# A hybrid streaming encoder step on one core: operands loaded into the low parts' place, norm scaled ahead of its copies, one partial kept over each change of phase, sums built further apart

## The chip, the cores and the metric

The kernel runs on one core of one Trainium2 chip. The metric is device time in microseconds of one execution; lower is better. All inputs, weights and results are float32.

## The reference, cut to what matters

```python
def layer(x, pool_buf, conv_buf, offset, ...):
    h = rmsnorm(x, norm_g)                       # x: 1024 + 64 tokens, D = 2048
    proj = einsum('btd,dc->btc', h, w_in)        # 2048 x 10240
    xa, za, v, bg, cg, zb, ga, gb = split(proj)  # 6 x 1024, 2 x 2048 columns
    ya, new_pool = pool_mixer(xa, ...)           # trailing means, small linear map
    ya = ya * silu(za)
    yc, new_conv = conv_mixer(cg * v, ...)       # three taps
    yb = bg * yc * silu(zb)
    merged = sigmoid(ga + b) * (ya @ w_proj_pool) + sigmoid(gb + b) * (yb @ w_proj_conv)
    return x + merged @ w_out, new_pool, new_conv
y = rmsnorm(layer(x), final_norm_g)
```

## The kernel before

All large products have the tokens on the free axis: weights are the stationary operand, activations (feature on the partition, 1,088 tokens) the moving one. To reach float32 accuracy each matrix is split into a high part (rounded to the fast float32 format) and a low part (the rest), and a product is three matmuls: high by high, high by low, low by high.

**Seven products for eight.** The work goes in pairs, numbered g = 0 to 111. A pair is 256 output columns by 1,024 (8 x 128) rows of weights. It is treated as a 2 x 2 block product and computed with seven block products instead of eight (q = 0 to 6), whose operands are sums and differences of blocks. So there are 784 products, s = 7g + q. A product is 24 matmuls of 272 tokens; in the last two phases 12 matmuls of 384.

**Phases.** H0 (g 0 to 39) and H1 (40 to 79) are the two halves of the input projection's rows: H0's results are partial sums, stored to memory (`part`) and loaded again in H1. H1's pairs also carry the pooling, convolution and gate work. YA (80 to 87) and YB (88 to 95) are the two branch projections, M0 (96 to 103) and M1 (104 to 111) the two halves of the output projection for the first 768 tokens, again with a partial result in memory (`part_m`). A tail T of 64 products of 12 matmuls of 320 tokens does the last 320 tokens without the seven-for-eight scheme.

**Operands of a phase.** The seven moving operands of a phase stand in SBUF as `ops` (H0 to YB) or `opm` (M0, M1), each with a high and a low half. At a change of phase they are all replaced, while the last pair of the old phase still uses them one by one. Three are plain blocks (`rawq`), four are sums (`sumq`) which "builds" make ahead of time: SyncE loads a quarter into `tb_in`, VectorE makes four differences into `tb_out` (`build`), GpSimd stores them; each build waits for the store of the one before. At the change SyncE loads operand o into one of two staging buffers (`load_operand`, `stage` or `stm`), ScalarE rounds it into the high half (`operand_hi`, L927), VectorE subtracts into the low half (`operand_lo`, L1171). The load of operand o + 2 waits for the low part of operand o:

```python
if o < 2:
    sp.wait_ge(tb_stored, 16 * BUILT[YB if ph == YA else ph])
    sp.wait_ge(ops_lo, NQ * (ph - 1) + NQ)
else:
    sp.wait_ge(ops_lo, k - 1)
```

**Order of the work.** Every engine runs one list, written by hand, in order of s. At position s ScalarE drains product s - 1 if it is its turn, and makes the high part of the weights of product s + 3; VectorE drains product s - 1 (L1164, all seven of a pair in H1 and M1, three in the others), makes the low part of the weights of s + 3 (L1118) and the weight sum of s + 4 (L1137), then whatever else is scheduled there. TensorE starts product s when its weights are split, its operand is there, and product s - 2 is drained. SyncE issues nearly all loads in one list of its own, GpSimd the stores. Each waits in order: whoever waits holds up all behind it.

**Buffers.** Three 8.7 KB-per-partition result buffers `pb` form a ring, `ring(g)`: g mod 3 up to H1, then g mod 2; `pbm` has two in M0 and M1. A buffer may be written when the store of its last content has landed. In YA and YB the third one holds gates (`gate`).

**The start.** For each of nine token tiles ScalarE squares the rows (L1050), VectorE makes the variance (L1394), GpSimd the inverse root (`rstd`), VectorE scales (L1401), TensorE turns the tile (L802, 16 transposes into four PSUM areas), ScalarE copies the first half out (`copy_first`, L1043) and VectorE the second (`copy_second`, L1389). Both copies of tile t stand ahead of the scaling of tile t + 1. Then come the first operands: `first_operand_sum`, `first_operand_hi`, `first_operand_lo` (L1184, L939, L1188).

**The end.** In M1 each pair's result is turned back (`turn_back`), added to x (`sum_columns`) and squared (`square_columns`, six squares of ScalarE at position q = 4), and at q = 5 of four pairs a quarter of the last tokens' operand `opb` is rounded (L1079) and subtracted (L1435). After product 783 SyncE loads the last rows of x (`res`), the final norm's vector (`fin_g`), and then goes on with the weights of T.

Of the kernel before, what the change touches and what calls it, by code (L numbers as in the profile page):

```python
# [10 lines left out]
P = 128  # L11
# [4 lines left out]
def bass_hybrid_stream_step(nc, x_prompt, x_sample, state_pool, state_conv, norm_g, w_in, b_gate,  # L16
# [25 lines left out]
    KQ = 4  # L42
# [58 lines left out]

    def ring(g):
        return g % 3 if g < FIRST[YA] else g % 2

    stored_after, n_stored = {}, [0, 0, 0]
    for g in range(FIRST[M1]):
        ph, j = phase(g), g - FIRST[phase(g)]
        if ph == H1:
            k = {"gate": 1, "za": 2, "zb": 2}.get(KIND[j], 0)
        else:  # L110
            k = {H0: 1, YA: 1, YB: 3, M0: 1}[ph]
        n_stored[ring(g)] += 16 * k
        stored_after[g] = n_stored[ring(g)]

    with ExitStack() as ctx:
# [31 lines left out]
        ops = at("ops", 0, [NQ, KQ, 2, TH], F32R)  # L147
        pb = [at(f"pb{k}", PB0 + k * PB_B, [2, TOK]) for k in range(3)]
# [23 lines left out]
        t0 = at("t0", PB0 + KE * TOK * 4, [KQ, TH])  # L172
# [4 lines left out]
        opm = at("opm", 0, [NQ, KQ, 2, AH], F32R)  # L177
        opb = at("opb", OPM_B, [KD, 2, B], F32R)
        PBM0 = OPM_B + KD * 2 * B * 4
        pbm = [at(f"pbm{k}", PBM0 + k * 2 * A * 4, [2, A]) for k in range(2)]  # L180
        assert PBM0 + 2 * 2 * A * 4 <= PB0 + 2 * PB_B
        xcol = [at(f"xcol{k}", (PB0 + 2 * PB_B, DS0)[k], [AT, 2 * P]) for k in range(2)]
        sqj = at("sqj", DS0 + AT * 2 * P * 4, [2 * P])
        stm = [at(f"stm{k}", (XE0, WS0)[k], [KQ, AH]) for k in range(2)]
        tbm_in = at("tbm_in", XE0, [4, AH])
        tbm_out = at("tbm_out", WS0, [4, AH])
        stb = [at(f"stb{k}", (XE0, WS0)[k], [KQ, B]) for k in range(2)]
        res = at("res", 0, [BT, D])
        ob = at("ob", BT * D * 4, [2, B])
        fin = [at(f"fin{k}", (BT * D * 4 + 2 * B * 4, WS0)[k], [D]) for k in range(2)]  # L190
        fin_g = at("fin_g", XE0, [D])
# [47 lines left out]
        def out_tile(g):  # L239
            return pb_first if g == 0 else pbm[g % 2] if g >= FIRST[M0] else pb[ring(g)]  # L240
# [8 lines left out]
        def operand(ph):  # L249
            return ops if ph < M0 else opm  # L250
# [42 lines left out]
        stage_landed = [sem(f"stage_landed{k}") for k in range(2)]  # L293
# [39 lines left out]
        stb_landed = [sem(f"stb_landed{k}") for k in range(2)]  # L333
# [69 lines left out]
        BUILD = [(FIRST[H0] + 4 + k, 3, H1, k) for k in range(KQ)]  # L403
        BUILD += [(FIRST[H1] + GB0 + 1 + k // 2, 2 + 3 * (k % 2), (YA, YB)[k // KQ], k % KQ) for k in range(2 * KQ)]
        BUILD += [(FIRST[YB] + 5 + k // 2, 2 + 3 * (k % 2), M0, k) for k in range(KQ)]
        BUILD += [(FIRST[M0] + 2 + k, 3, M1, k) for k in range(KQ)]
        BUILT = {ph: sum(p <= ph for _, _, p, _ in BUILD) for ph in range(6)}

        SOURCE = ((0, 0), (1, 0), (1, 1), (0, 3), (1, 2), (0, 2), (1, 3))

# [6 lines left out]
        for g in range(NP):  # L417
            if is_partial(g):
                n_landed[ring(g)] += 16
                landed_after[g] = n_landed[ring(g)]  # L420
# [13 lines left out]
        def _(sp):  # L434
# [19 lines left out]
            def load_partial(g):  # L454
                ph, j = phase(g), g - FIRST[phase(g)]
                if ph == H1:
                    before = g - 3
                    kind, i = (KIND[j - 3], (j - 3 - CONV0) // 4) if j >= 3 else ("gate", 0)
                    if kind == "xa":
# [7 lines left out]
                    sp.wait_ge(pb_stored[ring(j)], stored_after[j])  # L467
                    sp.dma_start(pb[ring(g)][:, :, :].rearrange("p c t -> p (c t)"), part[j]) \
                        .then_inc(pb_landed[ring(g)], 16)
                else:  # L470
                    if j < 2:
                        sp.wait_ge(pb_stored[ring(g)], stored_after[g - 2])
# [1037 lines left out]
```

## Time and profile before

| | |
|---|---|
| median of 3 runs | 2656.14 us (2653.65 to 2657.09) |
| the profiled execution | 2653.98 us |
| its span, first to last instruction | 2652.2 us |
| TensorE busy | 2487.2 us, 94% |
| VectorE, ScalarE, GpSimd busy | 1600.6, 888.3, 106.5 us |
| mean granted TensorE clock | 0.973 |
| DMA, mean over the span | 163 GB/s |

The span is what the trace covers; 1.8 us of the execution's time lie around it. TensorE's busy time contains stretches in which it ran at half its clock, so the distance to an undisturbed run is more than the 6% of idle time.

### The profile page before, as it was taken

How to read it: one execution, taken by the hardware profiler on the slowest of the kernel's cores; microseconds unless marked ns; L12 is line 12 of the kernel's file. 1: busy time of each engine (PE TensorE's matmuls, PEld its weight loads, DVE VectorE, ACT ScalarE, POOL GpSimd, SP SyncE). 2: the span in 40 equal slices, each digit the busy share in tenths (PEclk: the TensorE clock that was granted, in tenths of full speed). 3: DMA queues.
4: the chain of work that ended last, by engine and by line, in shares of the span. 5: the costliest groups of instructions: out<-in, count | busy, mean ns of one | idle time of the engine just before them, and what ended most of it. 6: DMA issues, size and time to landing. Idle time of an engine off the chain costs nothing.

```text
span 2652.2 us, 44708 instructions
## 1 busy us (share of the span) xinstructions
PE 2487.2 (94%) x18737; PEld 2474.6 (93%) x18737; DVE 1600.6 (60%) x2311; ACT 888.3 (33%) x1493; POOL 106.5 (4%) x201
## 2 busy tenths in 40 slices
PE   4799999999999989999999999889998996989987
PEld 3799999999999989999999999889998996989887
DVE  4745444444444476777777687666556666667654
ACT  4433333333333333323322222224334323444354
POOL 1000000000000000000000000000000010000000
PEclk9899999999999989999999999989999998989999
DMA  4345333333233444343333333785447585667686
GB/s 176 116 131 202 111 111 99 104 102 99 99 111 112 151 177 150 120 153 137 141 107 116 116 116 111 255 285 216 151 161 272 200 282 195 215 222 245 216 270 186
DMA packets 216013, 433.63 MB, mean 163 GB/s; under 512 B 9684, under 2 KB 168724, under 8 KB 196295
## 3 DMA queue, kind: packets, MB, share of 16 engines
q1 hardware_dynamic: 191222, 291.70, 33.1%
q0 software_dynamic: 23648, 132.27, 13.4%
q10 hardware_dynamic: 944, 6.82, 0.7%
q8 instruction: 149, 2.44, 0.4%
q14 instruction: 50, 0.40, 0.0%
HBM read 295.87 MB, written 134.88 MB: 162 GB/s over the span
## 4 chain that ended last, share of the span: by engine, by line
PE 81%; DMA 8%; DVE 6%; issue 3%; ACT 2%; POOL 0%; SPq 0%; DVEq 0%; ACTq 0%; POOLq 0%
PE ps L785 77%; DMA stage<-sumq 1%; DMA raw<-in_w_out_dram 1%; PE ps L886 1%; DMA stm<-sumq 1%; DMA sumq<-tb_out 1%; PE ps L802 1%; PE ps L815 1%; ACT ops L927 1%; DVE ops L1171 1%; DMA tbm_in<-rawq 1%; DMA tb_in<-rawq 1%; DVE xn L1401 1%; DVE tb_out L1208 1%; ACT sqj L1018 1%
## 5 line engine op out<-in xcount | busy, mean ns | idle before, releaser
L785 PE MATMUL ps<-ops,hi 128*128 128x272 f32 x10752 | 1807.4, 290 | 71.5 <-DVE pb L1164 53.5
L785 PEld LDWEIGHTS ps<-ops,hi 128*128 128x128 f32 x10752 | 1544.6, 191 | 75.3 <-issue 75.3
L785 PE MATMUL ps<-ops,lo 128*128 128x272 f32 x5376 | 1121.0, 290 | 0.0
L785 PEld LDWEIGHTS ps<-ops,lo 128*128 128x128 f32 x5376 | 847.5, 190 | 0.0
L1164 DVE TENSOR_TENSOR pb<-pb,ps 128x544 f32<-128x544 f32 x429 | 308.9, 720 | 382.6 <-PE ps L785 381.5
L907 ACT ACTIVATE hi<-sb 128x512 fp32r<-128x512 f32 x448 | 283.7, 633 | 637.7 <-PE ps L785 555.5
L1118 DVE TENSOR_TENSOR lo<-raw,hi 128x512 fp32r<-128x512 f32 x400 | 275.5, 689 | 298.0 <-ACT hi L907 295.8
L1118 DVE TENSOR_TENSOR lo<-sb,hi 128x512 fp32r<-128x512 f32 x448 | 308.2, 688 | 204.2 <-ACT hi L907 202.6
L907 ACT ACTIVATE hi<-raw 128x512 fp32r<-128x512 f32 x400 | 252.8, 633 | 480.5 <-PE ps L785 420.2
L920 ACT COPY pb<-ps 128x544 f32<-128x544 f32 x220 | 134.8, 613 | 416.0 <-PE ps L785 415.9
L785 PE MATMUL ps<-opm,hi 128*128 128x384 f32 x896 | 234.8, 343 | 27.2 <-DVE pbm L1164 17.3
L785 PEld LDWEIGHTS ps<-opm,hi 128*128 128x128 f32 x896 | 164.3, 193 | 30.7 <-issue 30.3
L1137 DVE TENSOR_TENSOR sb<-raw 128x512 f32<-128x512 f32 x224 | 153.4, 685 | 0.0
L785 PE MATMUL ps<-opm,lo 128*128 128x384 f32 x448 | 152.4, 340 | 0.0
L886 PE MATMUL ps<-opb,hi 128*128 128x320 f32 x512 | 115.9, 315 | 0.0
L886 PEld LDWEIGHTS ps<-opb,hi 128*128 128x128 f32 x512 | 86.6, 191 | 0.0
L785 PEld LDWEIGHTS ps<-opm,lo 128*128 128x128 f32 x448 | 86.1, 192 | 0.0
L886 PE MATMUL ps<-opb,lo 128*128 128x320 f32 x256 | 79.9, 312 | 0.0
L1137 DVE TENSOR_TENSOR sb<-sb,raw 128x512 f32<-128x512 f32 x112 | 76.7, 685 | 0.0
L1137 DVE TENSOR_TENSOR sb<-raw,sb 128x512 f32<-128x512 f32 x112 | 76.7, 685 | 0.0
L1171 DVE TENSOR_TENSOR ops<-stage,ops 128x2176 fp32r<-128x2176 f32 x21 | 50.9, 2423 | 26.3 <-ACT ops L927 26.3
L802 PE MATMUL ps<-ident,xn 128*128 128x128 f32 (+1 forms) x144 | 30.7, 406 | 32.3 <-DVE xn L1401 32.3
(121 smaller groups left out, 1030.7 us busy)
## 6 DMA issues: line engine op xcount, KB each, us to landing
raw<-in_w_in_dram SPq DMA_DIRECT2D x160, 512.0 KB, 3.8
pb<-part SPq DMA_DIRECT2D x40, 1088.0 KB, 6.8
part<-pb POOLq DMA_DIRECT2D x39, 1088.0 KB, 5.0
raw<-in_w_out_dram SPq DMA_DIRECT2D x64, 512.0 KB, 4.4
gates<-pb POOLq DMA_DIRECT2D x16, 1088.0 KB, 8.7
gate<-gates SPq DMA_DIRECT2D x32, 544.0 KB, 8.3
tb_in<-rawq SPq DMA_DIRECT2D x12, 1088.0 KB, 8.1
sumq<-tb_out POOLq DMA_DIRECT2D x12, 1088.0 KB, 9.6
```

What stands on the lines that cost most here:

```text
L785: mm = nc.tensor.matmul(ps[b][:, c, 0:n], w[:, s % R, kt * P:(kt + 1) * P], t[:, q, kt, half, k * n:(k + 1) * n], start=fresh and kt == 0 ...
L802: mm = nc.tensor.transpose(flat[b][:, k * P:k * P + r], xn[0:r, t, (a * KE + k) * P:(a * KE + k + 1) * P], ident[0:r, 0:r])
L815: mm = nc.tensor.matmul(ps[3][:, jb, 0:HC], w[:, kt, jb * P:(jb + 1) * P], ds[:, kt, half, :], start=kt == 0 and w is mix_hi and half == 0 ...
L886: mm = nc.tensor.matmul(ps[0][:, cb % 2, 0:B], w[:, n % R, kt * P:(kt + 1) * P], opb[:, kq * KQ + kt, half, :], start=kq == 0 and kt == 0 ...
L907: nc.scalar.activation(split_of(hi, n), src, ACT.Copy).then_inc(w_hi, 1)
L920: nc.scalar.copy(target(s), psum(s)).then_inc(act_drained, 1)
L927: nc.scalar.copy(operand(ph)[:, o, :, 0, :], (stage if ph < M0 else stm)[slot][:, :, :]) \
L1018: nc.scalar.activation(sqj[:, :], xcol[j % 2][:, t, :], ACT.Square, accum_out=sums_a[:, t, j:j + 1]).then_inc(squared, 1)
L1118: nc.vector.tensor_tensor(split_of(lo, n), src, f32(split_of(hi, n)), ALU.subtract).then_inc(w_lo, 1)
L1137: nc.vector.tensor_tensor(sb_of(g, q), a, b, op).then_inc(s_made, 1)
L1164: nc.vector.tensor_tensor(target(s), target(s), psum(s), ALU.add).then_inc(dve_drained, 1)
L1171: nc.vector.tensor_tensor(t[:, o, :, 1, :], src, f32(t[:, o, :, 0, :]), ALU.subtract).then_inc(ops_lo, 1)
```

## The change

1. **Operands load into place.** The staging buffers go. `ops_raw[o]` and `opm_raw[o]` are float32 views of the operands' own memory, and an operand is loaded where its low half will stand (rows of 544 or 384 values, one out of two). Its load waits only for the old phase's product o, and the last operand's load for the last product. Rounding starts four positions after, the subtraction, now in place, five: one operand at each position (`HI_LAG`, `LO_LAG`). `opb` is done in the same manner.
2. **The start.** `variance` of tile t + 1 stands ahead of the scaling of tile t, and the copies of tile t - 2 behind it; the first operand is rounded and subtracted before the last tile's copies, whose tokens it does not hold. The second and third operands' sums get memory of their own, so that one need not wait for the use of the other. The stores of `h1raw` start with the tokens that are ready.
3. **One partial kept.** The last pair of H0 and of M0 computes the same columns as the first of H1 and M1 (`position`, `is_kept`), and its result stays in its buffer instead of going out and in. `ring` is shifted to fit: g mod 3 in H0, (g - 1) mod 3 in H1, and it starts at 0 in YA, YB and M0. `pbm` moves to other memory.
4. **Builds further apart.** The eight builds of YA and YB stand 5 products apart (before 3 and 4 in turn), those of M0 4 apart (before 3 and 4). `tb_in` and `tb_out` have other places in M1.
5. **The end.** The six squares are spread in twos over q = 4, 5, 6, the rounding of `opb` moves to q = 1, `fin_g` is loaded in M1, the last rows from the second product of the last pair on.

```diff
     def ring(g):
-        return g % 3 if g < FIRST[YA] else g % 2
+        ph = phase(g)
+        if ph in (H0, H1):
+            return (g - (ph == H1)) % 3
+        return (g - FIRST[ph] + (ph == M1)) % 2
...
+        BUILD = [(NQ * (FIRST[H0] + 4 + k) + 3, H1, k) for k in range(KQ)]
+        BUILD += [(NQ * (FIRST[H1] + GB0 + 1) + 2 + 5 * k, (YA, YB)[k // KQ], k % KQ) for k in range(2 * KQ)]
+        BUILD += [(NQ * (FIRST[YB] + 5) + 4 * k, M0, k) for k in range(KQ)]
+        BUILD_LOAD_AT = {max(s - 3, BUILD[e - 1][0] + 1 if e > 0 else 0): e for e, (s, _, _) in enumerate(BUILD)}
+        HI_LAG, LO_LAG = 4, 5
...
             def load_operand(ph, o):
+                if o == 0:
+                    sp.wait_ge(tb_stored, 16 * BUILT[ph])
+                sp.wait_ge(product_done, NQ * (FIRST[ph] - 1) + o + 1)
                 kind, i = SOURCE[o]
+                sp.dma_start(operand(ph)[1][o][:, :, 1, :], (sumq if kind else rawq)[ph][:, i, :, :]) \
+                    .then_inc(ops_landed[o], 16)
...
+            def load_last_rows():
+                sp.wait_ge(product_done, NS - NQ + 2)
...
                 if q == 0:
+                    if g == FIRST[M0]:
+                        act.wait_ge(tb_made, 4 * BUILT[M0])
+                    elif stored_before[g] > 0:
+                        act.wait_ge(pb_stored[ring(g)], stored_before[g])
...
+            variance(0)
+            dve.wait_ge(g_landed, 16)
+            for t in range(TT):
+                if t + 1 < TT:
+                    variance(t + 1)
                 dve.wait_ge(rstd_made, t + 1)
                 nc.vector.scalar_tensor_tensor(xn[0:r, t, :], ...).then_inc(x_scaled, 1)
+                if t > 1:
+                    copy_second(t - 2)
```

VectorE's list at the start of the program, before the change (`xn` is the tile, `h1raw` the second half's copy out of PSUM):

```order
3 L1394 TENSOR_SCALAR var<-ssq 128x1
4 L1401 SCALAR_TENSOR_TENSOR xn<-xn,rstd,gbc 128x2048
5 L1394 TENSOR_SCALAR var<-ssq 128x1
6 L1389 COPY h1raw<-ps 128x8x128
7 L1401 SCALAR_TENSOR_TENSOR xn<-xn,rstd,gbc 128x2048
```

And VectorE's list at the same place with the change:

```order
3 L1419 TENSOR_SCALAR var<-ssq 128x1 x2
4 L1429 SCALAR_TENSOR_TENSOR xn<-xn,rstd,gbc 128x2048
5 L1419 TENSOR_SCALAR var<-ssq 128x1
6 L1429 SCALAR_TENSOR_TENSOR xn<-xn,rstd,gbc 128x2048
7 L1419 TENSOR_SCALAR var<-ssq 128x1
8 L1429 SCALAR_TENSOR_TENSOR xn<-xn,rstd,gbc 128x2048
9 L1414 COPY h1raw<-ps 128x8x128
```

Three tiles are scaled ahead of the first copy, where before a copy stood between any two; the second variance now stands ahead of the first scaling.

SyncE's list around the change from H0 to H1, before the change (`stage` are the staging buffers, `raw` the weights, `pb` the partial results):

```order
18 L490 DMA stage_63<-rawq 128x2176
19 L490 DMA stage_64<-sumq 128x2176
20 L447 DMA raw<-in_w_in_dram 128x4x256
21 L468 DMA pb_51<-part 128x2176
22 L490 DMA stage_63<-sumq 128x2176
23 L490 DMA stage_64<-rawq 128x2176
24 L447 DMA raw<-in_w_in_dram 128x4x256
25 L490 DMA stage_63<-sumq 128x2176
26 L490 DMA stage_64<-rawq 128x2176
27 L490 DMA stage_63<-sumq 128x2176
```

And SyncE's list at the same place with the change (`ops_raw` are the operands' own places):

```order
18 L516 DMA ops_raw_50<-rawq 128x4x544
19 L516 DMA ops_raw_51<-sumq 128x4x544
20 L516 DMA ops_raw_52<-sumq 128x4x544
21 L475 DMA raw<-in_w_in_dram 128x4x256
22 L516 DMA ops_raw_53<-rawq 128x4x544
23 L516 DMA ops_raw_54<-sumq 128x4x544
24 L516 DMA ops_raw_55<-rawq 128x4x544
25 L475 DMA raw<-in_w_in_dram 128x4x256
26 L498 DMA pb_58<-part 128x2176
27 L516 DMA ops_raw_56<-sumq 128x4x544
```

The load of pair 40's partial (21 before) is gone; each operand load stands behind one product of the old phase instead of the low part two before it, is made of rows of 544 values instead of one run of 2,176, and the last one stands behind the load of pair 41's partial.

## Rows read from the trace of the kernel before

**Rows 1.** The chain that ended last, four of its pieces: start, length, what.
```profile
111.52 809.35 PE ps L785 x6432
...
926.47 6.26 DMA stage<-sumq
932.75 2.02 ACT ops L927
...
2507.11 15.27 DMA raw<-in_w_out_dram
```

**Rows 2.** Stretch of M0, L785 alone: length, PE busy (matmuls), clock, DMA share, GB/s.
```profile
2247.00:2340.00 93.00, 93.00 (x537) 1.00 0.61 205
```

**Rows 3.** As rows 2, for L886, two stretches of the tail T.
```profile
2505.00:2534.00 29.00, 17.34 (x102) 0.82 0.84 278
2534.00:2563.00 29.00, 28.67 (x191) 1.00 0.95 284
```

**Rows 4.** TensorE's waits: us in total, times, longest.
```profile
PE ps L785 <- DVE pb L1164: 53.5, 14, 10.3
```

**Rows 5.** As rows 2, stretches with waits in them.
```profile
929.00:965.00 36.00, 26.65 (x177) 0.81 0.66 240
1671.00:1790.00 119.00, 103.46 (x760) 0.91 0.77 275
1829.00:1868.00 39.00, 30.41 (x225) 0.96 0.72 257
2016.00:2048.00 32.00, 23.16 (x169) 0.89 0.70 247
2160.00:2225.00 65.00, 49.59 (x355) 0.87 0.79 282
2226.00:2247.00 21.00, 11.12 (x50) 0.76 0.32 111
2348.00:2380.00 32.00, 20.25 (x90) 0.79 0.74 249
2402.00:2473.00 71.00, 62.13 (x342) 1.00 0.65 223
```

**Rows 6.** The timeline of the start: start, length, instruction, idle before it.
```profile
13.77 1.91 ACT L1050 ACTIVATE junk<-xn 128x2048 f32<-128x2048 f32 x1 [5.81 <-DMA xn<-in_x_prompt_dram]
...
24.86 1.23 DVE L1389 COPY h1raw<-ps 128x1024 f32<-128x1024 f32 x1 [3.71 <-PE ps L802]
26.00 2.34 DVE L1401 SCALAR_TENSOR_TENSOR xn<-xn,rstd,gbc 128x2048 f32<-128x2048 f32 x1
...
28.40 3.68 PE L802 MATMUL ps<-ident,xn 128*128 128x128 f32 x16 [3.58 <-DVE xn L1401]
...
78.73 1.25 PE L785 MATMUL ps<-ops,hi 128*128 128x272 f32 x4 [5.50 <-DVE ops L1188]
```

**Rows 7.** The page: costliest groups (busy, mean ns) and DMA issues (us to landing).
```profile
L1164 DVE TENSOR_TENSOR pb<-pb,ps 128x544 f32<-128x544 f32 x429 | 308.9, 720 | 382.6 <-PE ps L785 381.5
...
L1118 DVE TENSOR_TENSOR lo<-sb,hi 128x512 fp32r<-128x512 f32 x448 | 308.2, 688 | 204.2 <-ACT hi L907 202.6
...
L1171 DVE TENSOR_TENSOR ops<-stage,ops 128x2176 fp32r<-128x2176 f32 x21 | 50.9, 2423 | 26.3 <-ACT ops L927 26.3
...
gates<-pb POOLq DMA_DIRECT2D x16, 1088.0 KB, 8.7
...
tb_in<-rawq SPq DMA_DIRECT2D x12, 1088.0 KB, 8.1
sumq<-tb_out POOLq DMA_DIRECT2D x12, 1088.0 KB, 9.6
```

**Rows 8.** Stretches of all engines: PE, PEld, DVE, ACT, POOL busy; clock, DMA share, GB/s.
```profile
10.00:15.00 5.00, 1.31 (x7) 1.20 (x7) 2.84 (x4) 1.23 (x1) 0.56 (x1) 1.00 1.02 424
...
194.00:201.00 7.00, 7.00 (x58) 7.00 (x57) 4.87 (x8) 1.56 (x3) 0.20 (x1) 1.00 0.87 269
```

**Rows 9.** The timeline of TensorE in pair 107 of M1.
```profile
2420.05 0.59 PE L785 MATMUL ps<-opm,hi 128*128 128x384 f32 x2 [1.40 <-DVE pbm L1164]
```

More of the change, by code:

```diff
@@ L147, in bass_hybrid_stream_step @@
         ops = at("ops", 0, [NQ, KQ, 2, TH], F32R)
+        ops_raw = [at(f"ops_raw{q}", q * KQ * 2 * TH * 4, [KQ, 2, TH]) for q in range(NQ)]
         pb = [at(f"pb{k}", PB0 + k * PB_B, [2, TOK]) for k in range(3)]
@@ L164, in bass_hybrid_stream_step @@
         so = at("so", DS0, [E])
+        tb_in = {ph: at(f"tb_in{ph}", XE0 if ph < M1 else WS0, [4, TH if ph < M0 else AH])
+                 for ph in (H1, YA, YB, M0, M1)}
+        tb_out = {ph: at(f"tb_out{ph}", WS0 if ph < M1 else DS0, [4, TH if ph < M0 else AH])
+                  for ph in (H1, YA, YB, M0, M1)}
         xn = at("xn", 0, [TT, D])
@@ L239, in out_tile @@
         def out_tile(g):
-            return pb_first if g == 0 else pbm[g % 2] if g >= FIRST[M0] else pb[ring(g)]
+            return pb_first if g == 0 else pbm[ring(g)] if g >= FIRST[M0] else pb[ring(g)]
         def target(s):
@@ L249, in operand @@
         def operand(ph):
-            return ops if ph < M0 else opm
+            return (ops, ops_raw) if ph < M0 else (opm, opm_raw)
         V_B, V_S, V_W = 0, 2 * KD, 2 * KD + KE
@@ L292, in bass_hybrid_stream_step @@
         ops_lo = sem("ops_lo")
-        stage_landed = [sem(f"stage_landed{k}") for k in range(2)]
+        ops_landed = [sem(f"ops_landed{k}") for k in range(NQ)]
         tb_landed = sem("tb_landed")
@@ L417, in bass_hybrid_stream_step @@
         for g in range(NP):
-            if is_partial(g):
+            if is_partial(g) and not is_kept(g - 1):
                 n_landed[ring(g)] += 16
@@ L454, in load_partial @@
             def load_partial(g):
-                ph, j = phase(g), g - FIRST[phase(g)]
+                ph, j = phase(g), position(g)
                 if ph == H1:
                     before = g - 3
-                    kind, i = (KIND[j - 3], (j - 3 - CONV0) // 4) if j >= 3 else ("gate", 0)
-                    if kind == "xa":
+                    kind, i = (KIND[j - 3], (j - 3 - CONV0) // 4) if j >= 3 else (None, 0)
+                    if j < 3:
+                        sp.wait_ge(pb_stored[ring(g)], stored_after[g - 4])
+                    elif kind == "xa":
                         sp.wait_ge(dve_drained, dve_count[NQ * before + 6])
@@ L622, in _ @@
-            sp.wait_ge(product_done, NS)
-            for t in range(BT):
-                sp.dma_start(res[0:rows(AT + t), t, :], x_rows(AT + t)).then_inc(res_landed, 16)
-            sp.wait_ge(opb_lo, KQ)
-            sp.dma_start(fin_g[:, :], final_norm_g.rearrange("(a d) -> a d", a=1).broadcast_to([P, D])) \
-                .then_inc(fin_g_landed, 16)
+                if q == 0:
+                    load_weights(2 * g + 3)
+                    if ph == M1:
+                        load_x_columns(j)
+                    if ph == H1 and j < CONV0 and j % 4 == 1:
+                        load_mix(j // 4)
+                    if g + 1 < NP and is_partial(g + 1) and not is_kept(g):
+                        load_partial(g + 1)
@@ L682, in store_pair @@
             def store_pair(g):
-                ph, j, k = phase(g), g - FIRST[phase(g)], ring(g)
+                ph, j, k = phase(g), position(g), ring(g)
+                if is_kept(g):
+                    return
                 if ph == H0:
@@ L1011, in input_post, with square_columns @@
                                 .then_inc(conv_tails, 1)
-            def square_columns(j):
+            def square_columns(j, tiles=range(AT)):
                 act.wait_ge(summed, 2 * j + 2)
-                for t in range(AT):
+                for t in tiles:
                     if AT * j + t > 0:
@@ L1389, in copy_second, with variance @@
                 nc.vector.tensor_copy(h1raw[:, :, t * P:t * P + r], src).then_inc(h1_copied, 1)
-            for t in range(TT):
+            def variance(t):
                 r = rows(t)
```

311 lines of the change are left out of this document (148 added, 163 removed).

## The prediction, made before the changed kernel was run

> **What bounds the kernel now.** I read the time table first: TensorE is busy 94% of the span, so the kernel is TensorE's work plus what TensorE loses. Then the chain of work that ended last: from 111.52 us on it is one piece of 809.35 us of TensorE, 6,432 matmuls, so an undisturbed matmul of 272 tokens costs 809.35 / 6,432 = 0.1258 us and a product of 24 costs 3.02 [rows 1]. In M0 an undisturbed matmul costs 93.00 / 537 = 0.1732, a product 2.08 [rows 2], in the tail 29.00 / 191 = 0.152 with its transposes [rows 3]. Third, TensorE's waits: 53.5 us in 14 waits for a result to be drained [rows 4]. They stand at few places, so I took stretches around them and counted matmuls. What a stretch is longer than its matmuls' undisturbed time is its loss, waits and slow clock together [rows 5]:
>
> - H0 to H1, 929 to 965: 36 - 177 x 0.1258 = 13.7
> - builds for YA and YB, 1671 to 1790: 119 - 95.6 = 23.4
> - H1 to YA: 39 - 28.3 = 10.7
> - YA to YB: 32 - 21.3 = 10.7
> - builds for M0 and the change to M0: 65 - 44.7 = 20.3 and 21 - 50 x 0.1732 = 12.3, together 32.6
> - M0 to M1: 32 - 15.6 = 16.4
> - M1, pairs 106 to 109: 71 - 59.2 = 11.8
> - start of T: 29 - 102 x 0.152 = 13.5 [rows 3]
>
> The clock is in these numbers: in the first stretch the engine was idle 36 - 26.65 = 9.35 us, yet 13.7 were lost; the granted clock of the stretch was 0.81, that is, part of it stood at 1.2 GHz instead of 2.4 after the waits. I price a wait of some us at its length plus 2 us.
>
> **The start.** Now each tile is a cycle: scaling 2.34, turning 3.68, copy 1.23, one after the other, so that TensorE idles 3.58 before each 3.68 of turning [rows 6]: 7.26 us a tile, nine tiles. With two scalings ahead, turning and VectorE's work (about 3.6 a tile) overlap and the turning bounds, say 3.74. Against that, the second variance now stands ahead of the first scaling, and needs tile 1: its squares start at 13.77, when the tile lands, and take 1.91 and some 0.2 to read the sum out [rows 6]. So the first scaling ends near 18.3, the nine turns (the last one half as long) near 50. VectorE is then still at: two copies to 50, a weight sum and the first operand's low part to 53, five weight steps of 0.6 and the last copy to about 57, where product 0 starts; now it starts at 78.73 [rows 6]. Products 1 to 6 come at the pace of the operands in both versions: per operand a rounding 2.0, a low part 2.42 and a sum 2.4. Walking both engines' new lists with these durations, I get products 1 to 6 at 66, 71, 75, 82, 86, 90; the present chain has product 6 at 111.52 [rows 1]. **Gain 22.** Bounds: 15, if the turns run 0.5 slower and the operands' order costs a wait, to 26.
>
> **Changes of phase.** Now staging, rounding and low part form a chain: 6.26 for the load, 2.02, 2.42 [rows 1, 7]: 10.7 for every second operand. That chain goes. Next is VectorE: in seven positions in a row it has a low part 2.42, a weight low part 0.69, 4/7 of a weight sum, and 6/7 of a drain 0.72 [rows 7], about 3.9 us with the overlap of issue, against 3.02. The list allows it about 2 us of lateness (a low part is made two positions ahead: 6.0 - 3.9). So 7 x 3.9 - 7 x 3.02 - 2 = 4 us of waiting, plus 2 to 2.5 of clock: **6.5 for H0 to H1, gain 7.2.**
>
> The loads themselves: each consists of 512 rows of 2,176 bytes. No load before has that destination; the nearest is `tb_in`, with rows of the same length. Alone with little else it had 269 GB/s at a busy share of 0.87, so 309 when full; whole rows moved at 424 [rows 8]. Seven operands, two weight loads, a partial in and one out are 11.1 MB: 26 us at 424 GB/s, 36 at 309. From the first load to the need for the last low part there are 12 products, 36.1 us, less 6.4 for latency, rounding and low part: 29.7, and with VectorE's stall 33.7. So at the fast rate nothing is added, at the slow one 2 to 6 us at each of three changes. I take 0, as both queues together had 282 GB/s averaged over 65 us with pauses in it [rows 5], and keep 6 for the range. The Trainium skill, page "DMA: Bandwidth & Descriptors", section "Where 436 GB/s comes from", says that for HBM to SBUF the HBM side binds at about 358 GB/s per core. By that, 11.1 MB would take 31 us and each of three changes about 1 us more, the result some 3 us later than mine. The 424 GB/s of the row stands against it as a hard bound.
>
> **H1 to YA: gain 0.** Here the new `ring` puts pair 80 into the buffer of pair 79 (before: of 78). ScalarE's first drain in YA must wait for pair 79's gates to be stored. From the start of pair 80: VectorE is 2.4 late, drain 0.7, sigmoid of 1,088 values 1.2 (as the copy of 1,024 values [rows 6]), issue 0.5, store 8.7 to landing [rows 7]: 13.5. Product 2 needs the drain at 6.0: 7.5 of waiting plus 0.6, 0.6 and the clock 2: 10.7, what is lost now. Behind this drain ScalarE holds roundings and weights of the next products, but those have slack. From a gain of 5 (the store lands after 5 us) to a loss of 5.
>
> **YA to YB: gain 5.2.** As H0 to H1, with three drains but two merges of 1.2: 5.5 remain.
>
> **Builds: gain 20.4.** Each waits for the store of the one before, 9.6 us, and for its own load, 8.1, which starts only when the one before is made [rows 7]. With 2.7 for the build and 0.6 to issue that is a cycle of 13 to 14; it stood 9.05 and 12.1 apart and will stand 15.1 apart. 3 us are left for some load that stands behind a pair's weights and partial in SyncE's list.
>
> **M0: gain 20.1.** Builds 12.1 apart with a cycle of 13.2 (smaller rows): three times 1.2 late, 3 in all. At the change, VectorE has low parts of 1.7, four merge steps of 1.2, two drains, weights: 25.3 us against 2 x 3.02 + 5 x 2.08 and 4 of slack, by position 6.7, plus 2 to 3 of clock. The wait of ScalarE's first drain for the last store of YB goes, since `pbm` moves. 12.5 remain of 32.6.
>
> **M0 to M1: gain 9.1.** VectorE 3 us a position against 2.08: 4.8 of waiting, 2.5 of clock: 7.3 remain.
>
> **M1: gain 5.6.** Four waits of 1.40 [rows 9], in which the low part of `opb` waited for six squares and a rounding. Six other microseconds there are the turns back, which stay. **T: gain 12.** Now the weights stand behind `res` and `fin_g` and take 15.27 to land [rows 1]. Then `res` is issued a pair's half earlier, `fin_g` long before; I leave 1.5, as ScalarE needs these weights within about 9 us.
>
> The kept partials save two stores and two loads, which nothing waited for: 0.
>
> **Sum:** 22 + 7.2 + 0 + 5.2 + 20.4 + 20.1 + 9.1 + 5.6 + 12 = 101.6. The profiled execution took 2653.98; less 101.6 that is 2552.4. The median of the runs lies 2.2 above it: **2554**.
>
> **Rivals.**
> - *The phase changes are bound by the loads.* For it: the rate of `tb_in`, and that seven loads now crowd into 30 us. Against: the 424 GB/s. It gives 6 more at three changes and 3 at the two of M0 and M1: 2578. Chance 0.18.
> - *TensorE hardly waits at the changes.* If VectorE's slack is larger than 2 us, only the gate store and a little remain, 17 instead of 42.5: 2529. Against it: a position's 3.9 us are sums of measured durations. 0.09.
> - *The builds' cycle stays late.* If loads and stores, with operands and gates beside them, take 13 us and not 10, each of twelve builds is still 1 to 3 late and the loads of the phase after with them: 2554 + 20 + 15 = 2589. 0.06.
> - *Slower.* The loads into place, one queue, do not overlap: 8.1 each [rows 7]. Seven then take 57 against 30, 27 of waiting at five changes, 135 plus clock against the 42.5 of my sum: 2657, no change; with the 9.6 of `sumq` 37 each, 2709. It decides for slower from about 8.3 us a load. Against it: 282 GB/s over 65 us is 4 us for 1.1 MB. 0.03, and 0.02 for the point between.
> - My forecast, 2536 to 2570: 0.62.
>
> **Range and chances.** 2536 to 2584 holds my case and most of the first rival. A change of 0.2%, 5 us, is about what a measurement of this kernel tells from none. Only the last rival reaches that: faster 0.95, same 0.02, slower 0.03.
>
> **What the profile after would show.** Product 0 near 57 us, product 6 near 90. At H0 to H1 no staging loads in the chain, VectorE without gaps, waits of TensorE under 5 us. At the start of YA one wait of 6 to 8 us, ScalarE behind the gates' store. No wait over 2 us in the builds' pairs. In M1 no waits of 1.40. No 12 us gap at the second block of T. I am wrong if ScalarE's roundings wait for `ops_raw` (first rival), or if new waits stand in T when its first one no longer gives the loads time.

## The result, and the profile of the changed kernel

The changed kernel took 2591.05 us (2586.20 to 2592.78, 4 runs), the kernel before beside it 2654.89 us (2646.17 to 2657.09, 4 runs): a ratio of 0.9767, 95% interval 0.9752 to 0.9781. That is faster by 2.3%, and 37 us later than forecast, outside the range. The profiled execution took 2591.84, its span is 2590.1 against 2652.2 before: 62.1 us less, where the sum had 101.6. Of all runs below one, of experiment 8, took 4011.94 us at a granted clock of 0.558 in place of 0.99, and is left out of its median.

First the stretches that answer to those of [rows 2, 3, 5], for the matmuls of the products (L812, before L785) and then for those of the tail (L913, before L886); the columns are length, TensorE busy (matmuls), TensorE's weight loads, clock, DMA share, GB/s:

```profile
897.00:945.00 48.00, 44.83 (x351) 44.06 (x351) 1.00 0.68 254
1642.00:1762.00 120.00, 111.76 (x854) 111.19 (x854) 0.96 0.72 259
1781.00:1836.00 55.00, 46.69 (x351) 46.11 (x350) 0.91 0.65 242
1967.00:2018.00 51.00, 42.75 (x307) 42.07 (x306) 0.90 0.81 300
2101.00:2180.00 79.00, 68.13 (x511) 67.53 (x509) 0.94 0.80 282
2180.00:2204.00 24.00, 17.95 (x82) 17.00 (x83) 0.86 0.55 194
2219.00:2286.00 67.00, 59.57 (x340) 58.37 (x339) 1.00 0.59 204
2300.00:2342.00 42.00, 33.26 (x175) 31.35 (x175) 0.96 0.74 254
2357.00:2421.00 64.00, 60.72 (x339) 57.91 (x337) 1.00 0.70 251
...
2453.00:2482.00 29.00, 25.75 (x168) 24.53 (x168) 1.00 0.98 309
```

Each length less its matmuls at 0.1258, 0.1732 or 0.152 us, as in the prediction, gives the loss:

| place | lost before | forecast | lost after | gain forecast | gain found |
|---|---|---|---|---|---|
| start, to product 6 | | | | 22 | 20.2 |
| H0 to H1 | 13.7 | 6.5 | 3.8 | 7.2 | 9.9 |
| builds for YA, YB | 23.4 | 3 | 12.6 | 20.4 | 10.8 |
| H1 to YA | 10.7 | 10.7 | 10.8 | 0 | -0.1 |
| YA to YB | 10.7 | 5.5 | 12.4 | 5.2 | -1.7 |
| builds for M0, and the change | 32.6 | 12.5 | 14.7 + 9.8 | 20.1 | 8.1 |
| builds for M1 | 0 [rows 2] | 0 | 8.3 | 0 | -8.3 |
| M0 to M1 | 16.4 | 7.3 | 11.7 | 9.1 | 4.7 |
| M1, four pairs | 11.8 | 6.2 | 5.3 | 5.6 | 6.5 |
| start of T | 13.5 | 1.5 | 3.5 | 12 | 10.0 |
| sum | | | | 101.6 | 60.1 |

So some 41 us of the forecast are missing, and nearly all of it stands at builds and at three changes of phase (YA to YB, to M0, to M1). What ends last there is seen in the chain that ended last (start, length, what):

```profile
91.28 821.40 PE ps L812 x6528
...
1668.78 13.24 DMA tb_in<-rawq
1689.68 12.31 DMA tb_in<-rawq
...
1808.29 8.10 DMA gates<-pb
...
1993.28 11.84 DMA ops_raw<-sumq
...
2109.51 12.30 DMA tb_in<-rawq
...
2161.27 13.28 DMA opm_raw<-rawq
...
2222.19 5.78 DMA tb_in<-rawq
...
2321.91 10.17 DMA opm_raw<-sumq
```

One piece of TensorE now reaches from 91.28, in the first pair, to 912.68, in the last pair of H0; before it reached from 111.52 to 920.87 [rows 1]. At the change into H1 the chain goes through VectorE's work alone, with no load. At the later changes and the builds it goes through loads of 6 to 13 us. Only the `gates` store was foreseen. What stands ahead of two of them in SyncE's list is read from the timeline, first at the first pair of YB, with ScalarE's rounding that waits for the load:

```profile
1991.83 0.37 SPq L475 DMA_DIRECT2D raw<-in_w_proj_conv_dram  x1
1992.30 0.45 SPq L550 DMA_DIRECT2D gate<-gates  x1
1992.85 0.38 SPq L562 DMA_DIRECT2D ma<-part_a  x1
1993.28 0.43 SPq L516 DMA_DIRECT2D ops_raw<-sumq  x1
...
2005.14 2.02 ACT L953 CAST ops<-ops_raw 128x2176 fp32r<-128x2176 f32 x1 [5.27 <-DMA ops_raw<-sumq]
```

and at a build of pair 75:

```profile
1688.72 0.37 SPq L475 DMA_DIRECT2D raw<-in_w_in_dram  x1
1689.19 0.45 SPq L498 DMA_DIRECT2D pb<-part  x1
1689.68 0.53 SPq L539 DMA_DIRECT2D tb_in<-rawq  x1
...
1702.02 1.36 DVE L1233 TENSOR_TENSOR tb_out<-tb_in 128x544 f32<-128x544 f32 x2 [5.76 <-DMA tb_in<-rawq]
```

The wanted load was issued within 1.5 us of three or two others and landed 11.84 and 12.31 us later. ScalarE then stood 5.27 us and VectorE 5.76 us, each with drains of TensorE's results behind it in its list.

The first of these loads was also issued late. TensorE had done the old phase's last product, and with it the place was free, at 1983.63; the load went out at 1993.28, 9.7 us after. What SyncE waited for in between (who, for whom; us in total, times, longest):

```profile
SPq L475 <- DVE sb L1161: 9.3, 1, 9.3
```

L475 is the load of the new pair's weights, which stands ahead in the list and waits until VectorE has made the weight sums out of the same buffer. So being behind another load has two prices: the wait of that load, which holds up SyncE's whole list, and the time in which its bytes move.

### The profile page after: what moved, and what is told of

It is laid out like the page before. It is cut to its first block, busy times and chain, and to the rows that moved or that the text cites. A ratio compares the mean times of both kernels' runs of the same rounds, so it can differ in the third digit from the quotient of the medians.

```text
span 2590.1 us, 44672 instructions
## 1 busy us (share of the span) xinstructions
PE 2469.5 (95%) x18737; PEld 2455.7 (95%) x18737; DVE 1600.4 (62%) x2311; ACT 889.1 (34%) x1493; POOL 119.7 (5%) x199
## 3 DMA queue, kind: packets, MB, share of 16 engines
q0 software_dynamic: 23360, 130.37, 13.7%
## 4 chain that ended last, share of the span: by engine, by line
PE 82%; DMA 7%; DVE 7%; issue 3%; ACT 1%; SPq 0%; DVEq 0%; POOL 0%; ACTq 0%; POOLq 0%
PE ps L812 77%; DMA tb_in<-rawq 3%; PE ps L913 3%; DVE sb L1161 1%; DVE lo L1142 1%; PE ps L842 1%; DVE ops L1196 1%; DVE tb_out L1233 1%; DMA opm_raw<-rawq 1%; DVE xn L1429 1%; DVE pb L1191 1%; ACT hi L934 1%; DMA ops_raw<-sumq 0%; DMA ops_raw<-rawq 0%; DMA raw<-in_w_out_dram 0%
## 5 line engine op out<-in xcount | busy, mean ns | idle before, releaser
L812 PE MATMUL ps<-ops,hi 128*128 128x272 f32 x10752 | 1806.1, 290 | 51.1 <-DVE pb L1191 23.6
L812 PEld LDWEIGHTS ps<-ops,hi 128*128 128x128 f32 x10752 | 1541.3, 191 | 55.0 <-issue 47.7
L812 PE MATMUL ps<-ops,lo 128*128 128x272 f32 x5376 | 1120.8, 290 | 0.0
L812 PEld LDWEIGHTS ps<-ops,lo 128*128 128x128 f32 x5376 | 847.5, 190 | 0.0
L812 PE MATMUL ps<-opm,hi 128*128 128x384 f32 x896 | 233.9, 342 | 25.9 <-DVE pbm L1191 16.8
L812 PEld LDWEIGHTS ps<-opm,hi 128*128 128x128 f32 x896 | 162.8, 191 | 30.8 <-issue 30.2
L812 PE MATMUL ps<-opm,lo 128*128 128x384 f32 x448 | 151.9, 339 | 0.0
L913 PE MATMUL ps<-opb,hi 128*128 128x320 f32 x512 | 114.3, 312 | 0.0
L812 PEld LDWEIGHTS ps<-opm,lo 128*128 128x128 f32 x448 | 85.6, 191 | 0.0
L913 PEld LDWEIGHTS ps<-opb,hi 128*128 128x128 f32 x512 | 85.1, 188 | 0.0
L913 PE MATMUL ps<-opb,lo 128*128 128x320 f32 x256 | 79.2, 309 | 0.0
L1191 DVE TENSOR_TENSOR pbm<-pbm,ps 128x384 f32<-128x384 f32 x80 | 44.2, 552 | 17.3 <-PE ps L812 17.0
L712 POOL DMA_DIRECT2D part<-pb x38 | 20.3, 534 | 728.5 <-ACT pb L948 728.5
```

Of the source, the lines that this page charges most:

```text
L712: pool.dma_start(part[j], out_tile(g)[:, :, :].rearrange("p c t -> p (c t)")).then_inc(pb_stored[k], 16)
L812: mm = nc.tensor.matmul(ps[b][:, c, 0:n], w[:, s % R, kt * P:(kt + 1) * P], t[:, q, kt, half, k * n:(k + 1) * n], start=fresh and kt == 0 ...
L913: mm = nc.tensor.matmul(ps[0][:, cb % 2, 0:B], w[:, n % R, kt * P:(kt + 1) * P], opb[:, kq * KQ + kt, half, :], start=kq == 0 and kt == 0 ...
L1191: nc.vector.tensor_tensor(target(s), target(s), psum(s), ALU.add).then_inc(dve_drained, 1)
```

## The experiments

Losses below are by pair: from a pair's first matmul to the next pair's, less seven undisturbed products (3.013 us, 2.08 in M0 and M1). For the changed kernel they are: pair 40 4.1; 75 6.3; 77 6.1; 80 11.2; 87 and 88 together 12.7; 93 7.1; 94 2.5; 95 5.8; 96 9.6; 98 to 101 together 8.5; 103 and 104 together 11.9. The kernel before, run beside them 7 times each, took 2654.87 us (2651.91 to 2657.77) for experiments 1 to 4, 2651.59 (2647.67 to 2656.39) for 5, 6, 7 and 11, and 2653.38 (2651.07 to 2657.26) for 8, 9 and 10. Each ratio is to the runs beside it; where two kernels come from different groups, the ratios are the better comparison. Each has 4 runs, experiment 8 has 3.

**1. The last operand ahead of the other loads (x1_loads_first).**

```
                 if q == 0:
+                    if H0 < ph and j == 0:
+                        load_operand(ph, NQ - 1)
                     load_weights(2 * g + 3)
...
-                if ph in (YA, YB) and q < 2:
-                    load_gate((ph - YA) * NOUT + j, q)
+                if ph in (YA, YB) and q in (2, 3):
+                    load_gate((ph - YA) * NOUT + j, q - 2)
```

> The changed kernel (2591.05 us) with SyncE's list reordered alone: the last operand of a phase is loaded ahead of the weights, columns and partial of the new pair, and the gates of YA and YB are loaded two products later (q = 2 and 3). Theory A, a late load is late because of what stands ahead of it in SyncE's list: the losses of pair 88 (10.2 us) and 104 (10.5) fall to 5 or 6 each, that of pair 93, where a build's load stands behind two gate loads, from 7.1 to 1, pair 96 loses 2 less: 2575, 16 less. Theory B, the 16 DMA engines are full around the changes and every order costs the same: 2588 to 2594, with the waits moved to the gates (the merges of YA and YB) or the weights.

Measured: 2574.25 us (2572.10 to 2578.44), ratio 0.9699 (0.9685 to 0.9714): 17 less, as expected. Pair 88 (with 87) loses 6.3 in place of 12.7, pair 104 (with 103) 6.3 in place of 11.9, pairs 94 and 95 0.4 in place of 8.3. Pair 93 stayed at 7.3, and 96 at 10.2.

The edit moves two things, and the trace tells them apart. M1 has no gates, so what pair 104 gained, 5.7 us, is the last operand's. Its load took 9.82 us to land, hardly less than the 10.17 before; but it went out as soon as the last product was done, and not 6.9 us after. At pair 88 it even took 17.10 us in place of 11.84, but went out at once and not after 9.7: it no longer stands behind the wait of the weights' load. The 7.8 us of pairs 94 and 95 are the gates'. The first operand of M0 had stood behind weights and four loads of gates and `ma`, took 13.28 us (2161.27 in the chain above) and kept ScalarE waiting for 6.66; now it stands behind the weights alone, took 6.47, and nothing waits for it.

**2. The builds' loads earlier (x2_build_loads).**

```
-BUILD_LOAD_AT = {max(s - 3, BUILD[e - 1][0] + 1 if e > 0 else 0): e for e, (s, _, _) in enumerate(BUILD)}
+BUILD_LOAD_AT = {max(s - (3 if e in (0, 4, 12) else 6), BUILD[e - 1][0] + 1 if e > 0 else 0): e for e, (s, _, _) in enumerate(BUILD)}
```

> The changed kernel with the builds' loads issued right after the build before has been made (six positions ahead at most, instead of three); the first build of H1, YA and M0 keeps its place. Theory A: the losses at pairs 75 and 77 (6.3 and 6.1 us) go, and those of 98 to 101, the M1 builds (0.9, 2.4, 2.5, 2.7 us), too: 2591 - 12 - 8 = 2571. The loss at 93 stays, since its load stands there already. Theory B, loads and stores of builds are bound by the engines' rate: the loads come 9 us earlier but land as late, 2588 to 2594.

Measured: 2575.68 us (2575.18 to 2577.18), ratio 0.9704 (0.9689 to 0.9718), 15 less. The losses of pair 75 and of pairs 98 to 101 are gone. The load for pair 75 went out 5.0 us earlier, at 1684.72, and took 7.74 us in place of 12.31. Pair 77 still lost 5.6 and pair 93 7.1.

**3. The ring turned in YA, YB and M0 (x3_ring),** so that pair 80's result doesn't go into the buffer of pair 79.

```
-        return (g - FIRST[ph] + (ph == M1)) % 2
+        return (g - FIRST[ph] + (ph != M1)) % 2
...
-pbm = [at(f"pbm{k}", (XE0, PB0 + PB_B)[k], [2, A]) for k in range(2)]
+pbm = [at(f"pbm{k}", (PB0 + PB_B, XE0)[k], [2, A]) for k in range(2)]
```

> The changed kernel with the result ring of YA, YB and M0 turned by one, so that YA's first pair writes the buffer of pair 77 and not that of pair 79, whose gates are still being stored; nothing else. If the wait of 7.5 us in product 2 of YA is that store alone: pair 80 loses 4 instead of 11.2 us, 2584. Rival: the operands' loads and VectorE are as late as that store, and the wait only changes its name: 2589 to 2593.

Measured: 2589.19 us (2587.12 to 2590.06), ratio 0.9752 (0.9736 to 0.9769): against 0.9767 that can't be told from nothing. ScalarE's timeline at pair 80, first of the changed kernel, where the first drain waits for the store:

```profile
1816.42 0.61 ACT L948 COPY pb<-ps 128x544 f32<-128x544 f32 x1 [6.52 <-DMA gates<-pb]
```

and of this one, where the drain came on time and the rounding of the last operand waits instead:

```profile
1821.52 2.01 ACT L954 CAST ops<-ops_raw 128x2176 fp32r<-128x2176 f32 x1 [3.13 <-DMA ops_raw<-sumq]
```

The stall went, and the next thing that was late took most of its place: pair 80 lost 8.7 instead of 11.2.

**4. All three together (x4_three).**

> The three edits together. Theory A: 2591 - 16 - 20 - 7 = 2548, up to 2556 if the last load of H1 to YA profits twice. Theory B, engines' rate: 2580 or more. What then remains at each change of phase should be VectorE's list: 4 to 7 us at pairs 40, 80, 88, 96 and 104.

Measured: 2551.54 us (2550.14 to 2554.43), ratio 0.9613 (0.9599 to 0.9628). Now the ring gives its 7 us: pair 80 loses 4.2 with the last operand early and the gates later as well, 11.0 with those alone (1), 8.7 with the ring alone (3). Left were 4.1 at pair 40, 5.4 at 77, 4.2 at 80, 6.9 at 88, 7.5 at 93, 10.4 at 96 and 6.6 at 103 and 104. For pair 93 the chain and VectorE's timeline of this kernel name another transfer than before:

```profile
2091.53 11.05 DMA sumq<-tb_out
...
2102.68 1.02 DVE L1234 TENSOR_TENSOR tb_out<-tb_in 128x384 f32<-128x384 f32 x2 [6.75 <-DMA sumq<-tb_out]
```

The load is early; what isn't is the store of the build before, 12 us ahead, through which `tb_out` becomes free.

**5. Builds 5 positions apart for M0, and each build's load first in its position (y2_builds, on top of 4).**

```
-BUILD += [(NQ * (FIRST[YB] + 5) + 4 * k, M0, k) for k in range(KQ)]
+BUILD += [(NQ * (FIRST[YB] + 4) + 3 + 5 * k, M0, k) for k in range(KQ)]
...
+                early = ph < M0
+                if early and s in BUILD_LOAD_AT:
+                    load_build(BUILD_LOAD_AT[s])
                 if q == 0:
```

The first two builds now wait only for the pairs whose rows they read, as the other pairs are not stored yet.

> The kernel x4_three, with the four sums of M0 begun 4 positions earlier (pair 92) and 5 positions apart instead of 4, and each sum's load ahead of the weights and partial issued at the same position. Pair 93 loses 7.5 us because VectorE waits for the store of the sum before it (11.05 us to landing against 12 between sums), pair 77 loses 5.4 because its load lands 12.9 us after issue, behind weights, a gates store and a partial. If that is all, both go: 2538.5. Rival: the transfers only change places, and a weights load or a later sum is late instead: no more than 5 us gained, 2547 or more.

Measured: 2537.99 us (2536.89 to 2538.12), ratio 0.9568 (0.9553 to 0.9582). Pair 93 loses nothing, pair 77 2.7. This is the fastest of all the kernels, 53 us below the changed one.

**6. Half the bytes of every operand load (y1_half, on top of 4)** (this kernel leaves out half of the rows of each operand after H0: the loaded half is used twice, and the low parts are zero; ScalarE and VectorE process as many elements as before).

```
-                sp.dma_start(operand(ph)[1][o][:, :, 1, :], (sumq if kind else rawq)[ph][:, i, :, :]) \
+                sp.dma_start(operand(ph)[1][o][:, 0:2, 1, :], (sumq if kind else rawq)[ph][:, i, 0:2, :]) \
```

> The kernel x4_three, with each operand load cut to half its rows (two of four blocks of 128 partitions x rows; the rounding reads the loaded half twice, the low part is made from the rounded part alone and so is zero; both engines process as many elements as before). What the losses at the phase changes of x4_three are due to: if the loads' rate sets them (about 2.7 us a load, with weights, gates and stores between), the halved loads take most of them away: pair 40 from 4.1 to 1, pair 80 from 4.2 to 1, pair 88 from 6.9 to 1.5, pairs 96 and 104 from 10.4 and 5.4 to 3 and 1.5: 2530. If VectorE's work per position sets them (my terms in the prediction: low part, weight low part, sum and drain against a product), nothing changes but noise: 2551.

Measured: 2547.97 us (2546.31 to 2550.40), ratio 0.9606 (0.9588 to 0.9625), against 0.9613 of experiment 4. Pairs 40, 80 and 104 lose what they lost (4.1, 4.2, 5.4), pair 88 4.4 in place of 6.9, pair 96 8.4 in place of 10.4. So the loads' rate costs nothing at three changes and about 2 us at two.

**7. Rounding and low part one position later (y4_lags, on top of 4).**

```
-        HI_LAG, LO_LAG = 4, 5
+        HI_LAG, LO_LAG = 5, 6
```

> The kernel x4_three, with the rounding and the low part of each operand one position later (HI_LAG 5, LO_LAG 6), which gives each load 3 us more and VectorE one position of lateness less before TensorE waits. If late loads set the losses at the changes: about 3 us less at each of four of them, 2542. If VectorE's work sets them: about 3 us more at each, 2562.

Measured: 2564.92 us (2563.54 to 2567.88), ratio 0.9672 (0.9656 to 0.9688), 13 more than experiment 4, 16 by the ratios. Pairs 39 and 40 together lose 6.5 (4.1), 79 and 80 8.2 (4.2), 87 and 88 9.0 (6.9), 95 and 96 11.9 (10.4). More time for the loads made nothing better; less slack for VectorE made each change worse. That is what VectorE's work predicts.

**8. The low parts one position earlier (z2_lo4):** LO_LAG 4 on top of experiment 10.

> The kernel z1_start, with each low part of an operand one position earlier (LO_LAG 4 in place of 5, the rounding as it was). y4_lags took one position of slack from VectorE and lost 1.5 to 4 us at each change; halved loads gave nothing at three of five changes. If VectorE's lateness is the cost, one position more gives up to 3 us at each change, less the 2 us that the first low part now waits for its rounding: 1 to 2 at each of five, 2529. If the loads are late as soon as the low parts are wanted earlier (they land 9 to 13 us after issue, and a rounding is due 9 us after it), VectorE waits for them with its drains behind it: 2536 or more.

Measured: 2540.80 us (2539.86 to 2543.86, 3 runs), ratio 0.9577 (0.9561 to 0.9593) against 0.9572: no gain. Changes moved both ways: 39 and 40 lose 4.0 (4.1), 95 and 96 8.9 (9.4), 79 and 80 7.3 (4.2), 103 and 104 6.4 (6.4). Neither side of the expectation is borne out alone. At pairs 39 and 40 the trace shows VectorE again without gaps from 910.8 on; TensorE stood four times there, 3.0 us in all, each time for one of VectorE's drains. So one position more moved what VectorE does late, but not how much it has to do. At pair 80 two engines held each other up: VectorE stood three times for ScalarE's roundings, 4.5 us in all, which it did not do in experiment 10, and ScalarE's sigmoids of the gates stood 4.9 us for VectorE's drains, where it was 1.9.

**9. Two of seven low parts on GpSimd (z3_pool):** those of operands 1 and 5, on top of experiment 10.

```
+nc.gpsimd.tensor_tensor(t[:, o, :, 1, :], t_raw[o][:, :, 1, :], f32(t[:, o, :, 0, :]), ALU.subtract)
```

> The kernel z1_start, with two of the seven low parts of each phase after the first (those of operands 1 and 5) made by GpSimd instead of VectorE. If VectorE's work per position sets what is lost at the changes (pairs 40, 80, 88, 96, 104: 4.1, 4.2, 5.4, 9.2 and 5.4 us in y2_builds), 4.8 us less of it before the products take most: 3 at each, 2521. Rival: GpSimd is too slow or is held up beside VectorE (a power of one column took 0.56 us alone and 2.59 beside a scaling of 2.34), so that product 1 or 5 waits for it or VectorE's drains grow: 2536 or later.

Measured: 2561.79 us (2559.97 to 2564.25), ratio 0.9654 (0.9639 to 0.9668), 22 more than without it; pair 40 loses 10.1 in place of 4.1. The rival held. From the timelines of both engines at pairs 39 and 40:

```profile
914.58 2.42 DVE L1223 TENSOR_TENSOR ops<-ops_raw,ops 128x2176 fp32r<-128x2176 f32 x1
915.29 6.46 POOL L707 TENSOR_TENSOR ops<-ops_raw,ops 128x2176 fp32r<-128x2176 f32 x1 [15.98 <-ACT ops L978]
916.91 0.71 DVE L1216 TENSOR_TENSOR pb<-pb,ps 128x544 f32<-128x544 f32 x1
917.55 4.75 DVE L1167 TENSOR_TENSOR lo<-sb,hi 128x512 fp32r<-128x512 f32 x1
...
922.22 0.68 DVE L1186 TENSOR_TENSOR sb<-raw,sb 128x512 f32<-128x512 f32 x1
```

VectorE's operation of 0.68 us took 4.75 and ended about half a microsecond after GpSimd's; the drain before it, with one operand in PSUM, took its usual 0.71 beside GpSimd. Handing over 2.42 us of work cost VectorE 4.1. The Trainium skill, page "SBUF — State Buffer", section "Who interferes with whom", says just this: a VectorE instruction with two SBUF inputs contends with a GpSimd instruction that reads SBUF, one with at most one SBUF input does not. The trace agrees in both halves. Who began first matters too: the low part at 914.58 has two SBUF inputs and was under way when GpSimd began, and it took its usual 2.42.

**10. The second variance behind the first scaling (z1_start, on top of 5).**

```
-                if t + 1 < TT:
+                if 0 < t and t + 1 < TT:
                     variance(t + 1)
...
+                if t == 0:
+                    variance(1)
```

> The kernel y2_builds, with the variance of the second tile behind the first tile's scaling on VectorE. In the trace of the changed kernel the first scaling began at 15.97, when the second tile's squares were summed, though its own variance was ready at 10.6; the second scaling waited for GpSimd until 18.77. The first scaling then begins near 11.4 and the second near 16.7: all that follows is 2 us earlier, 2536. Rival: the third scaling waits for the third tile's squares (23.3) as before, and nothing is gained: 2538.

Measured: 2540.17 us (2537.18 to 2542.10), ratio 0.9572 (0.9556 to 0.9588) against 0.9568: no gain, as the rival had it. VectorE's timeline of the start:

```profile
11.49 2.35 DVE L1437 SCALAR_TENSOR_TENSOR xn<-xn,rstd,gbc 128x2048 f32<-128x2048 f32 x1 [0.76 <-POOL rstd L693]
15.83 0.15 DVE L1427 TENSOR_SCALAR var<-ssq 128x1 f32<-128x1 f32 x1 [1.98 <-ACT junk L1080]
17.92 0.15 DVE L1427 TENSOR_SCALAR var<-ssq 128x1 f32<-128x1 f32 x1 [1.94 <-ACT junk L1080]
17.99 2.34 DVE L1437 SCALAR_TENSOR_TENSOR xn<-xn,rstd,gbc 128x2048 f32<-128x2048 f32 x1
```

The first scaling is 4.5 us earlier, but the second stands behind the third tile's variance, whose squares are ready at 17.9. Product 0 came 1.2 us earlier, at 54.35.

**11. The start alone, on the kernel before (y3_start_alone).** Only the order of scaling and copies, not that of the first operands.

```
+            variance(0)
+            dve.wait_ge(g_landed, 16)
             for t in range(TT):
+                if t + 1 < TT:
+                    variance(t + 1)
...
-                if t > 0:
-                    copy_second(t - 1)
+                if t > 1:
+                    copy_second(t - 2)
```

> The kernel before with one part of the change alone: the norm's scaling two tiles ahead of its copies on VectorE and the copies of ScalarE in the same order; the first operands' order stays as before. My term for the start was 22 us with the operands' order in it, and the trace of the changed kernel showed 20. If the cycle of a tile (7.3 us to about 3.5) is nearly all of it: 2635, product 0 near 58. Rival: the operands' new order carries a good part (the first operand no longer waits for the last tile), then this part alone gives 15 or less: 2640 or more.

Measured: 2634.21 us (2632.82 to 2637.55), ratio 0.9933 (0.9917 to 0.9949), 17 less than the kernel before; in the traces H1 begins at 927.88 against 947.75, 19.9 earlier. Product 6 starts at 92.10 here and at 91.28 in the changed kernel. So the tile's cycle is nearly all of the start's gain, and the operands' new order gives 0.8 us at most.

## Why the prediction failed

**The start: right.** Forecast product 0 near 57, found 55.41; product 6 near 90, found 91.28; 20.2 of 22, and experiment 11 puts it where the prediction did.

**Changes of phase: the mechanism right, one term too large, one missing.** VectorE without gaps was forecast, and it is what the timeline of pair 40 shows (kernel of experiment 10):

```profile
912.78 2.42 DVE L1204 TENSOR_TENSOR ops<-ops_raw,ops 128x2176 fp32r<-128x2176 f32 x1
915.11 0.71 DVE L1199 TENSOR_TENSOR pb<-pb,ps 128x544 f32<-128x544 f32 x1
915.75 0.68 DVE L1150 TENSOR_TENSOR lo<-sb,hi 128x512 fp32r<-128x512 f32 x1
916.35 0.68 DVE L1169 TENSOR_TENSOR sb<-raw,sb 128x512 f32<-128x512 f32 x1
916.95 2.42 DVE L1204 TENSOR_TENSOR ops<-ops_raw,ops 128x2176 fp32r<-128x2176 f32 x1
919.28 0.68 DVE L1150 TENSOR_TENSOR lo<-sb,hi 128x512 fp32r<-128x512 f32 x1
919.89 0.68 DVE L1169 TENSOR_TENSOR sb<-raw 128x512 f32<-128x512 f32 x1
920.49 2.42 DVE L1204 TENSOR_TENSOR ops<-ops_raw,ops 128x2176 fp32r<-128x2176 f32 x1
922.82 0.71 DVE L1199 TENSOR_TENSOR pb<-pb,ps 128x544 f32<-128x544 f32 x1
```

One low part starts every 3.5 to 4.3 us, 3.8 on average over the six steps from 912.78 to 935.50, against my 3.9. The waiting of 4 us was right, but "plus 2 to 2.5 of clock" was not: TensorE's gaps at this change are now 0.3 to 1.7 us each, and the granted clock of 897:945 is 1.00, where before waits of some microseconds stood beside 0.81 [rows 5]. So 3.8 are lost and not 6.5. Experiments 6 and 7 bear the cause out: it isn't the loads' bytes, it is VectorE's work and its place in the list. In experiment 8 the loss of 4.0 stays although the low parts come earlier, as VectorE has no gap to use. That also settles the first rival, that the changes are bound by the loads' rate: about 2 us at two of five. Its sign did appear: ScalarE's roundings waited 2.7, 5.3, 6.7 and 6.5 us for a load at four of the changes. But another order of the loads, with the same bytes, brought the longest such wait from 5.3 to 2.8 us into YB, from 6.5 to 1.0 into M1, and from 6.7 to 4.1 into M0 (1).

What failed at YA to YB and M0 to M1 is the sentence on the loads themselves, "from the first load to the need for the last low part there are 12 products". It counts bytes against time and not the place in the list. The seventh operand's load stands behind the new pair's weights and, in YB, a gate and a part of `ma`, in M1 `x` columns and a partial; it could be issued when the old phase's last product is done, and ScalarE wants it three positions later. Behind the weights' wait it went out 9.7 and 6.9 us after that moment, and landed 11.84 and 10.17 us after issue. Experiment 1, which puts it first in its position, gave 6.4 and 5.7 us there; the 6.4 may hold a part of the gates, which moved too. Into M0 it was the first operand, behind four loads of gates and `ma`, that came late: 5.7 of the 15.4 us of pairs 93 to 95, of which 5.6 came back with the gates moved, while pair 96 lost 0.6 more.

**H1 to YA: right**, 10.8 against 10.7, by the wait that was named. What the prediction did not see is that the last operand's load stood right behind it, so that taking the store's wait away alone gives almost nothing (3), and 7 us in company (4).

**Builds: the step that failed most.** The forecast took 8.1 us for a load and 9.6 for a store [rows 7], medians over all builds, and found 15.1 us between builds to be enough. The store came mostly sooner than that (4.6 to 11.3 us for YA and YB, half of them within 6.4), but the cycle was not what bound: a load may be issued only three positions (9 us) ahead, and where this falls behind weights and a partial, with a store of gates on GpSimd's queue, as at pairs 74, 75 and 77, it goes out after them and then takes 12.3 to 13.5 us. "3 us are left for some load that stands behind a pair's weights and partial" named the case and took it for an exception; it was pairs 75 and 77 with 6.3 and 6.1 each and a good part of pairs 93 to 95, which lost 15.4 in all. The third rival, "the builds' cycle stays late", at 2589 and a chance of 0.06, is the one whose number came about, but the losses came by issue times and order more than by the cycle, so that the number fits is in part luck. The cycle of load and store itself bound only at pair 93 (4), where builds stand 12 us apart; there three times 1.2 was forecast, and 7.5 was lost.

**Builds for M1: a term left out.** I carried nothing for pairs 98 to 101. Before, the load of such a build stood in the list of the pair ahead. Now it is three products of 2.08 us, 6.2 us, ahead, and takes 5.8 to 6.9 us. Experiment 2 gives all 8.5 us back.

**M1 and T: sizes near,** 6.5 for 5.6 and 10.0 for 12. **Kept partials: 0**, as nothing in the trace waits there; no experiment was made on them alone, nor on the end (part 5 of the change), whose gains are read from the stretches.

Altogether experiments 1, 2, 3 and 5, which change order, time of issue and one choice of buffers, bring the changed kernel from 2591 to 2538, below the 2554 that was forecast with some of these losses in it. What they leave stands at pairs 40, 80, 88, 96 and 104, with 4.1, 4.2, 5.4, 9.2 and 5.4 us. At 40 and 80 the chain shows VectorE's work and no load. At 88 and 96 an operand's load still ends last (16.20 and 11.78 us to landing in the kernel of experiment 5), and halved loads took 2.5 and 2.0 us off in experiment 6; that the rest there is VectorE's is argued, not shown.

## What to carry to other kernels

When a change lets transfers start earlier, price each by its place in the issuing engine's list, not by its median time to landing. Ask first what the loads ahead of it wait for: here the weights' load held the last operand back by 7 to 10 us. Then ask what was issued just before it: here a 768 KB load for M0's sums took 4.8 us where nothing had been issued just ahead (2098.11), and 12.3 and 12.9 behind weights, gates and `ma` (2109.51 and 2137.72). Put the transfer with the nearest deadline first in its position, and check the wait that comes next before taking one away: two stalls in one place are worth little singly and 7 us together. Where the unit of time of a phase gets shorter (3.02 to 2.08 us here), distances given in positions shrink with it.

## What was not expected of the hardware

Operand loads with rows of 2,176 bytes, for which no row stood before, flowed near the 424 GB/s of [rows 8]: in the changed kernel two of them landed 2.75 us apart where they followed one another (ScalarE's roundings of them began at 1979.02, 1981.77 and 1984.58), which is 1.11 MB in about 2.75 us, 405 GB/s. The Trainium skill, page "DMA: Bandwidth & Descriptors", section "Where 436 GB/s comes from", has about 358 GB/s for HBM to SBUF; the trace differs, and this decides. GpSimd took 4.9 to 8.0 us, in six of them, for a low part that VectorE makes in 2.42, and held VectorE's operation of 0.68 us up for 4.1 us meanwhile (9).
